# The two token halves of a weight panel, one after the other instead of in turn

## The reference, cut to what matters

```python
x = x + 0.5 * swiglu(rmsnorm(x, g_ffa), w_ffa_in, w_ffa_out)      # 1024 -> 2 x 2816 -> 1024
x = x + mixer(rmsnorm(x, g_mix))      # layer 0: latent attention (MLA), layer 1: chunkwise mLSTM
x = x + 0.5 * swiglu(rmsnorm(x, g_ffb), w_ffb_in, w_ffb_out)
x = x + sigmoid(rmsnorm(x, g_ple) @ w_ple_gate) * (p @ w_ple_proj)
```

## Time and profile before

| | |
|---|---|
| median of the executions | 2850.88 us |
| span of the profiled execution | 2847.9 us |
| TensorE busy (matmuls / weight loads) | 2746.0 / 2578.7 us, 96% / 91% |
| VectorE, ScalarE, GpSimd busy | 1448.7, 674.3, 882.8 us |
| mean granted TensorE clock | 0.970 of full speed |
| read from HBM | 206.57 MB, 75 GB/s with the writes |

### The profile page before, as it was taken

The page is one execution under the profiler, slowest core; times in us unless marked ns, Lnnn a source line. Parts: engine busy times, 40 slices in busy tenths (PEclk is TensorE's granted clock), DMA queues, the critical chain, the costliest instruction groups (busy, mean ns, idle before and its releaser), DMA issues.

```text
span 2847.9 us, 49206 instructions
## 1 busy us (share of the span) xinstructions
PE 2746.0 (96%) x19103; PEld 2578.7 (91%) x19103; DVE 1448.7 (51%) x1615; ACT 674.3 (24%) x984; POOL 882.8 (31%) x424
## 2 busy tenths in 40 slices
PE   7999999899999899999998999999999999999998
PEld 7999999666666799999998999999987799999998
DVE  5555325666443475553256555324533475554236
ACT  3222112344332122221123222112121122222122
POOL 2333333000010233333333333333320043333332
PEclk9999999999999999999999999999996799999999
DMA  4222222212332122222222222223321122222222
GB/s 131 81 81 82 74 83 67 55 22 55 83 80 76 30 82 81 81 79 76 81 83 82 83 85 80 71 81 94 81 59 63 43 80 83 85 83 69 82 82 74
DMA packets 423789, 215.45 MB, mean 76 GB/s; under 512 B 54933, under 2 KB 420890, under 8 KB 423706
## 3 DMA queue, kind: packets, MB, share of 16 engines
q1 hardware_dynamic: 421206, 210.88, 25.9%
q10 hardware_dynamic: 2500, 3.50, 0.4%
HBM read 206.57 MB, written 7.76 MB: 75 GB/s over the span
## 4 chain that ended last, share of the span: by engine, by line
PE 90%; DVE 7%; issue 2%; ACT 0%; DMA 0%; ACTq 0%; DVEq 0%; POOL 0%
PE ps L1688 25%; PE ps L1690 25%; PE ps L1693 25%; PE ps L689 2%; PE ps L721 2%; PE ps L672 1%; PE ps L656 1%; DVE S L544 1%; PE ps L1190 1%; DVE PP L473 1%; PE ps L707 1%; PE ps L1205 1%; DVE st L466 1%; PE ps L1225 1%; PE ps L1216 1%
## 5 line engine op out<-in xcount | busy, mean ns | idle before, releaser
L1350 POOL TENSOR_TENSOR wlo<-raw,whi 128x1024 fp32r<-128x1024 f32 (+3 forms) x383 | 831.4, 2171 | 1473.1 <-ACT whi L1388 1473.1
L1688 PE MATMUL ps<-xh,whi 128*128 128x288 f32 x3568 | 770.3, 297 | 11.0 <-DVE xl L1515 7.3
L1690 PE MATMUL ps<-xl,whi 128*128 128x288 f32 x3568 | 768.3, 297 | 0.0
L1693 PE MATMUL ps<-xh,wlo 128*128 128x288 f32 x3568 | 768.0, 297 | 0.0
L1388 ACT ACTIVATE whi<-raw 128x1024 fp32r<-128x1024 f32 (+3 forms) x383 | 368.3, 962 | 1493.8 <-PE ps L1693 1482.0
L1688 PEld LDWEIGHTS ps<-xh,whi 128*128 128x128 f32 x3568 | 572.5, 189 | 12.8 <-issue 5.8
L1693 PEld LDWEIGHTS ps<-xh,wlo 128*128 128x128 f32 x3568 | 573.4, 189 | 0.0
L1690 PEld LDWEIGHTS ps<-xl,whi 128*128 128x128 f32 x3568 | 573.0, 189 | 0.0
L1688 PE MATMUL ps<-uh,whi 128*128 128x288 f32 x1408 | 302.7, 296 | 0.0
L1693 PE MATMUL ps<-uh,wlo 128*128 128x288 f32 x1408 | 302.7, 296 | 0.0
L1690 PE MATMUL ps<-ul,whi 128*128 128x288 f32 x1408 | 302.7, 296 | 0.0
(11 more groups left out here) (336 smaller groups left out, 2605.9 us busy)
## 6 DMA issues: line engine op xcount, KB each, us to landing
raw<-in_w_ffa_in SPq DMA_DIRECT2D x88, 512.0 KB
raw<-in_w_ffb_in SPq DMA_DIRECT2D x88, 512.0 KB
pages<-in_cache_ckv SPq DMA_DIRECT2D x128, 128.0 KB, 2.0
raw<-in_w_ffa_out SPq DMA_DIRECT2D x32, 384.0 KB
raw<-in_w_ffb_out SPq DMA_DIRECT2D x32, 384.0 KB
raw<-in_w_mlstm_in SPq DMA_DIRECT2D x24, 512.0 KB
raw<-in_w_ffa_out SPq DMA_DIRECT2D x32, 320.0 KB
raw<-in_w_ffb_out SPq DMA_DIRECT2D x32, 320.0 KB
```

The lines of the kernel that those rows point to most:

```text
L1350: pool.tensor_tensor(lo[:, 0:n, :], raw[:, p % RAW, 0:n, :], hi[:, 0:n, :].bitcast(F32), ALU.subtract).then_inc(wlo_ready, 1)
L1688: mm(out[:, q, :], hi[:, n, :], h0[:, q, :], start=first and n == 0, stop=False)
L1690: mm(out[:, q, :], hi[:, n, :], l0[:, q, :], start=False, stop=False)
L1693: ins = mm(out[:, q, :], lo[:, n, :], h0[:, q, :], start=False, stop=end)
```

## The change

The loop over the two token halves is moved from the inside to the outside of `products`. For a panel, all chunks and all three products are issued for the first half, into the first bank of the slot, and then all again for the second half, into the other bank. The number of matmuls, their operands and the panel's one `panel_used` stay. The chunk waits and the hooks stand in the first half only.

```diff
-                for n in range(n_chunks):
-                    if at and n in at:
-                        at[n]()
-                    if waits:
-                        waits(n)
-                    h0, l0 = half(mh(n)), half(ml(n))
-                    for q in (0, 1):
+                for q in (0, 1):
+                    for n in range(n_chunks):
+                        if at and n in at and q == 0:
+                            at[n]()
+                        if waits and q == 0:
+                            waits(n)
+                        h0, l0 = half(mh(n)), half(ml(n))
                         mm(out[:, q, :], hi[:, n, :], h0[:, q, :], start=first and n == 0, stop=False)
-                    for q in (0, 1):
                         mm(out[:, q, :], hi[:, n, :], l0[:, q, :], start=False, stop=False)
-                    end = last and n == n_chunks - 1
-                    for q in (0, 1):
-                        ins = mm(out[:, q, :], lo[:, n, :], h0[:, q, :], start=False, stop=end)
+                        ins = mm(out[:, q, :], lo[:, n, :], h0[:, q, :], start=False, stop=last and n == n_chunks - 1)
                 ins.then_inc(panel_used, 1)
```

## The result

Two executions of the changed kernel took 2876.97 and 2874.93 us, median **2875.95 us**, against 2850.88: a ratio of 1.0084, 95% interval 1.0055 to 1.0114. It is 25 us slower, within the range of the prediction (2857 to 2884) and 7 us above its middle.

The account below looks back on a forecast made before the run. TensorE's matmul pace and its waits were taken to bound the kernel. Pace 0, chunk waits 16.4 us and clock 2.6 made 19 us on a median of 2850.9, rounded down to 2869 us; range 2857 to 2884.

Parts of the forecast that it names:

- The pace: Steady matmul spacing on TensorE, 0.133 us each: the new order changes it by 0, ends -13 and +4 ns per matmul.
- the 13 ns: Part of a 133 ns full-clock matmul beyond its columns' 120 ns; thought to be the next weight load, same in either order.
- The chunk waits: Panels whose chunks arrive late, and the hook: more matmuls stand behind each wait, 16.4 us in all.
- layer 1's: First panel of layer 1: VectorE's last `xl` ends at 1527.26, so the sums come 2.7 us later.
- `mlstm_out`: First panel of that stage: GpSimd's last `gTl` is late, so the second panel begins 0.9 us later.
- the hook: In `mla_in`: reached after 18 matmuls instead of 36, 30 follow, 2.4 us, all on the path; VectorE's wait grows to 3.3.
- place 1: First panels of `mla_in`, `ffb0_in`, mLSTM gates, `ffb1_in`: late `xl` beside a GpSimd subtraction, 1.9 us each, 7.6 together.
- place 3: Program's first panel: 27 matmuls instead of six follow the late last chunk, 2.8 us; wait ahead of it about 3.8.
- The clock: Half clock behind the three long waits (program's first panel, hook, layer 1's first panel): up to 9 us, 2.6 taken.
- B: Faster rival: changing banks costs the 13 ns, so most of it falls away; about 2671 or 2795 us; 5%.
- C: Slower rival: accumulating into the bank just written adds 4 ns per matmul, about 2930 us; 5%.
- D: Rival: waits cost nothing, `xl` coming earlier and VectorE's lateness absorbing the rest; clock holds; 2851 to 2857 us; 7%.

Follow-up runs that it names:

- experiment 1: Changed kernel with the old order only in panels holding a chunk wait or hook: 2850.39 us; mirror image, kernel before with the new order only there: 2875.28 us.
- x9: Changed kernel with GpSimd's subtraction held at four stage starts, the hook moved back, and extra matmuls in the first panels of program and layer 1: 2859.20 us.
- x4: Changed kernel with extra matmuls into an unread bank ahead of the longest waits (program's first panel, layer 1's first panel, hook): 2876.10 us.
- x3, experiment 3: Changed kernel with GpSimd's subtraction for the next panel held at four stage starts until VectorE has made the eighth `xl`: 2863.68 us.
- experiment 5: Changed kernel with the hook of the last `mla_in` panel moved to the second half's chunk 4, 36 matmuls ahead and 12 behind: 2870.17 us.
- x10: Kernel before with the new order only in the first panel of each gate stage: 2845.22 us.
- experiment 7, x8: Kernel before with 64 extra matmuls into an unread bank in TensorE's 9.26 us wait ahead of L592: 2850.43 us.
- Experiment 8: New order only in two gate panels of the kernel before, 2845.22 us; old order there in the changed kernel, 2874.35; kernel before delayed by 100 matmuls, 2864.66.

## Why the prediction was right, and where a size was off

**The pace, taken as 0 of -13 to +4 ns.** Right: 827 matmuls in 110 us, and experiment 1 leaves five sixths of the matmuls in the new order without moving the time. The reason given for the 13 ns, the next matmul's weight load, was a guess that no run confirms; that they are of another making than the bank is shown.

**The chunk waits, 16.4 us.** Right term by term, read in kernels in which the clock held at the place: 1.9 four times (7.7 for 7.6), first panel 2.8 (x9) for 2.8, layer 1's 2.75 (x4, x9) for 2.7, `mlstm_out` 0.9 for 0.9, the hook 2.4 (x3, x4) for 2.4, and 0 in the gate and FFN output stages. Together 16.5. The cause named for place 1, a GpSimd subtraction beside the `xl`, is shown by experiment 3. That all of the hook is on the path is shown by experiment 5; VectorE's wait behind it, forecast at 3.3 us, is 3.31 in experiment 3, where the clock held, and 4.92 after. One step of place 3 was wrong without harm to its 2.8 us: the wait was to stand ahead of the last chunk alone, about 3.8 us. It measured 1.93 ahead of chunk 6 and 1.29 ahead of chunk 7, since GpSimd's subtraction held up the `xh` of chunk 6. That isn't the order's own, as x10 has the same with the old order there.

**The clock, 2.6 us out of up to 9.** This is the term that was mis-sized. Behind the three long waits it came to 2.5, 1.6 and 1.7 us, 5.8 together. The step that failed is the threshold read into the earlier trace rows: idles of 1.63 and 2.31 us kept the clock and 4.66 lost it, so short ones seemed safe. After, the first panel lost it behind waits of 1.93 and 1.29 us, x10 behind 2.00 and 0.88, while the hook's 3.38 us in x3 kept it and 3.39 in the changed kernel did not. No length of the last idle divides these, and in experiment 7 the clock fell in the midst of matmuls that followed one another without idle. What does decide it is open. For the four stalls of 1.64 us and the like, called the safe side, the clock did hold.

**What had no term.** 4.1 us of half clock at the projections and the end, against 2.2 won in attention and mLSTM, and an input that landed 0.8 us later: 2.7 net. 16.5 + 5.8 + 2.7 = 25.0 of the 25.2 us. That these parts net to so little, and that the time stayed inside the range with the clock term at over twice its size, is in part luck. Experiment 8 shows that the order in the gate panels doesn't cause the losses, and that the old order can have those of the second gate stage and the end; for the first projection (1.4 us) that is open.

**The rivals.** B and C fell with the window. D was wrong: the `xl` was as long as before, since what makes it long didn't move, as its counter-argument had it. Its first half becomes true by an edit to GpSimd.

## What to carry to other kernels

When a loop over halves goes outside a loop over chunks that arrive one by one, each wait comes earlier by the work that was moved behind it, and what counts is the work that stands behind the last wait: price it per place as (matmuls now behind) - (matmuls before behind), less the slack that the place had. A neighbour's long instruction may be harmless only because of that slack; look for the one that runs beside it, and move that. An edit worth a few microseconds is judged at its place, by the difference of the starts in two traces, since the clock in places with nothing edited moves the total by as much.

## What the runs showed of the hardware

An fp32r matmul of 288 and 320 columns with a weight load of its own costs its columns at 2.4 GHz plus 13.3 ns (133.3 and 146.7 ns); of 256 columns most cost 120 ns, and some less. At 288 columns it is the same in one bank 24 times running and with the bank changed each time. At half clock 288 columns take 240 ns, with nothing added.

VectorE's fp32r subtraction of 128 x 576 takes 0.82 us alone and 2.7 beside GpSimd's subtraction of 128 x 1024, an addition of 0.76 us takes 2.85 there, and the `xh` of 0.51 takes 2.63. What is added is no fixed amount: the subtraction and the additions end 0.61 or 0.62 us after GpSimd's instruction does, the `xh` 0.32 us, also where little of GpSimd's was left (1.45 us for the addition L410 in the earlier trace rows).

TensorE's granted clock differed between kernels at the same instructions behind the same idle (3.38 and 3.39 us; 2.05 and 2.05 us), and it fell once from 1.00 to 0.51 within a run of matmuls without idle (x8, 959 us). Matmuls with no other use, put into a wait, kept or brought back the full clock in each of the four places where they were tried; too many of them cost more than the clock gives.
